# Layer 1 of a two-layer diffusion backbone: queries and keys leave the projection already turned, values are projected first

## The chip, the core and the metric

The kernel runs on one core of one Trainium2 chip. The metric is the device time of one execution in microseconds (us). Five engines work on their own instruction streams and wait for each other by semaphores: TensorE (PE, matmuls and turns), VectorE (DVE), ScalarE (ACT), GpSimd (POOL, which here only issues DMAs) and SyncE (SP, which issues the loads of all large weights).

## The reference

One step of a backbone with two layers over 384 tokens of width 1024: 128 context tokens (tile t=0) and 256 latent tokens (tiles t=1 and t=2), the latter on a grid of 4 rows and 64 columns. Layer 0 runs grouped-query attention and an mLSTM side by side; layer 1 runs neighbourhood attention. Behind each follows a mixture of experts (32 experts, two a token). Everything is float32. The change is in layer 1's mixer, which in the reference is

```python
q, k, v = split(h @ w_in, 3)            # h: 384 x 1024, w_in: 1024 x 3072; 16 heads of 64
# context tokens: plain attention over the 128 context tokens
# latent tokens: one softmax over
#   s_win = q . k(window) * scale + bias[head, drow, dcol]    (4 rows x 16 columns around the query)
#   s_ctx = q . cached_k * scale                              (128 cached context keys)
o = p_win @ v(window) + p_ctx @ cached_v
x = x + gate * (o @ w_out)
# further outputs: new_na_k, new_na_v = k and v of the context tokens
```

`h` is the normed and modulated row of x, with the modulation from a linear map of the condition.

## The kernel before

All weights go through a ring of six places of 2 MB each; SP issues the loads in the order of the list `stream`, each as soon as the place's former user is done (`freed`). Both layers share one set of functions; an argument `l` says which layer it is. In every function each engine works its list strictly in order.

**Turns of the normed rows.** At the end of layer 0, VectorE adds the experts' output to x and norms row tile after row tile (`rows`, `combine`, `normed`), announcing each by `h_ready`. ScalarE does the squares for it (`finish_layer`). PE turns each tile by eight 128x128 transposes (`transpose_rows`, L509), and ScalarE copies them from two banks into `hT` (`copy_transposed`, L1035). ScalarE comes to these copies only when the squares of all three tiles are done, and PE begins the projection only when all three tiles are turned.

**Projection** (`project`, L528). Six chunks of 512 columns of `w_in`: two of queries, two of keys, two of values. For each chunk and each token tile a group of eight accumulating matmuls: the stationary operand is a 128x128 block of `hT`, the moving one 512 columns of weights. The groups go round over four banks (banks 2 to 5); VectorE copies the even ones, ScalarE the odd ones (`copy_projected`), into rows of `qkv[1]`: token in the partition, column along the row. The bias table is masked by VectorE between two of its copies (`window_bias`).

**Attention** (`attention`). Eight pairs of heads, three units a pair (one for each token tile), 24 units in a pipeline over four engines:
- `scores` on PE (L701): two heads, 128 queries against 128 keys (t=0) or 384 keys (cached, then latent).
- `find_max` on VectorE: for latent units the max over cached keys (L1271), then bias sum and max over the 256 latent keys of each head (L1576).
- exponentials on ScalarE (L1134), scaling by the sum on VectorE (`normalise`, L1588 and L1591).
- `turn_probs` on PE (L714), copy on ScalarE (L1124), `values` on PE (L737), heads out by VectorE (`take_heads`, L1601).

The scores need queries and keys with the head's dimension in the partition. So for every pair PE turns its queries (`turn_queries`, L670 and L672: three blocks; those of latent tokens by a matmul with the table `flip`, which also mirrors the 64 columns of each grid row) into bank 7, ScalarE scales and copies them to `qT` (L1111), PE turns the keys (`turn_keys`, L686: four blocks) into the same bank, and VectorE copies them to `kT` (L1274). For the first pair this stands ahead of all units; for pair j+1 the queries are turned behind the values of pair j's first unit, the keys behind those of its second. Eight pairs, so the last pair has no turns of a following one beside it. The heads of the latent tokens are mirrored back by `take_heads`.

**POOL's queue in layer 1**: 32 loads of the bias table behind the last `h_ready`, the cached keys when all rows are turned, the cached values when the projection is done (they go where `hT` was), then both outputs `new_na_k` and `new_na_v`, then what waits for the end of attention.

**Output projection** (`project_out`, L786) takes the heads, which lie turned already, as stationary operand.

Of the kernel before, what the change touches and what calls it, by code (L numbers as in the profile page):

```python
# [24 lines left out]
P = 128  # L25
# [46 lines left out]
for _name, _n in (("ident", 128), ("trif", 128), ("ones", 128), ("flip", 128), ("window", 64),  # L72
                  ("slot", 128), ("skip", 1), ("eps", 1), ("pair", 3)):
    KEEP[_name] = slice(_at, _at + _n)
    _at += _n
# [9 lines left out]
def tables():  # L85
# [8 lines left out]
    mirror = p - col + GRID_W - 1 - col  # L94
    keep[p, KEEP["flip"].start + mirror] = 1.0
# [25 lines left out]
def build(nc, a, o):  # L121
    ctx = ExitStack()
    with ctx:
# [27 lines left out]
        def small_cut(*shape):  # L151
# [5 lines left out]
            if len(shape) == 3:  # L157
# [9 lines left out]
        ident, trif, ones, flip = (keep[:, KEEP[n]] for n in ("ident", "trif", "ones", "flip"))  # L167
        h = area_h[:, :].rearrange("p (t d) -> p t d", t=NT)
        hT = area_t[:, :].rearrange("p (k n) -> p k n", k=KT)
        qkv = [area_q[:, 0:NT * AB_W].rearrange("p (t n) -> p t n", t=NT),  # L170
               area_q[:, :].rearrange("p (t n) -> p t n", t=NT)]
# [29 lines left out]
        qT = [v.rearrange("p (b n) -> p b n", b=2) for v in (area_h[:, 1536:2304], area_h[:, 0:768])]  # L201
        kT = [v.rearrange("p (b n) -> p b n", b=2) for v in (area_t[:, 0:1024], area_h[:, 768:1792])]
        na_k = area_h[:, 1792:2816]
# [50 lines left out]
            "pair_done", "qT_copied", "kT_copied", "scores_done", "max_ready", "prob_ready", "prob_scaled", "probT_done",  # L254
# [29 lines left out]
        FIRST = (0, 2, 1, 3)  # L284
        stream = [("ada", 0, c) for c in FIRST[0:2]] + [("in", 0, 0)] + [("ada", 0, c) for c in FIRST[2:4]]
# [4 lines left out]
        for l in range(2):  # L290
            if l:
                stream += [("in", 1, c) for c in range(NA_CHUNKS)]
# [3 lines left out]
        IN_CHUNKS = (AB_CHUNKS, NA_CHUNKS)  # L296
        IN_W = (AB_W, NA_W)
        PROJ0 = (0, AB_CHUNKS * NT)

# [7 lines left out]
        def freed(eng, n):  # L307
# [5 lines left out]
            if kind == "in":  # L313
                eng.wait_ge(S["proj_done"], PROJ0[l] + NT * (c + 1))
# [45 lines left out]
        def _(sp):  # L360
# [65 lines left out]
            for n in range(NUM["in", 1, 0], NUM["moe", 1, 0]):  # L426
                if n == NUM["in", 1, 1]:
# [8 lines left out]
        def _(pe):  # L436
# [75 lines left out]
            def project(l):  # L512

                for c in range(IN_CHUNKS[l]):
                    if l == 0 and c == 0:
                        project_first()
                        continue
                    n = NUM["in", l, c]
                    w = min(512, IN_W[l] - 512 * c)
                    pe.wait_ge(landed[place(n)], when(n))  # L520
                    for t in range(NT):
                        g = PROJ0[l] + NT * c + t
                        if c == 0:
                            pe.wait_ge(S["trans_copied"], 2 * (NT * 2 * l + t + 1))
                        if g >= 4:
                            pe.wait_ge(S["proj_copied_act" if g % 2 else "proj_copied_dve"], (g - 4) // 2 + 1)
# [4 lines left out]
                    if l == 0:  # L531
                        ada_step(("in", c))

            def mlstm():

                for n in range(2 * NT):
# [6 lines left out]
                    for hh in range(B_HEADS):  # L543
                        c0 = (BK if side else BQ) + hh * BD
                        mm = pe.transpose(banks[3 + side][:, hh * P:hh * P + P], qkv[0][:, t, c0:c0 + BD], ident)
# [41 lines left out]
                def number_products(v, d):  # L587
                    pe.wait_ge(S["amatT_copied"], v + 1)
                    for hh in range(B_HEADS):
                        mm = pe.matmul(banks[5][:, hh * P:hh * P + P], amatT[:, hh, :],  # L590
                                       qkv[0][:, STAGES[s][d], BV + hh * BD:BV + hh * BD + BD], start=True, stop=True)
# [3 lines left out]
                for s in range(3):  # L595
# [28 lines left out]
                    if s < 2:  # L624

                        for d in range(2):
                            pe.wait_ge(S["kw_ready"], v + d + 1)
                            for hh in range(B_HEADS):
                                mm = pe.matmul(banks[(3, 0)[d]][:, hh * P:hh * P + P], kw[d][:, hh, :],
                                               qkv[0][:, STAGES[s][d], BV + hh * BD:BV + hh * BD + BD],  # L630
# [21 lines left out]
            def turn_queries(l, j):  # L652

                if l == 0 and j == 0:
                    pe.wait_ge(S["kdup_ready"], 1)
                    pe.wait_ge(S["ctx_v"], 16)
                if l == 1 and j == 0:
                    for name in ("proj_copied_dve", "proj_copied_act"):
# [1377 lines left out]
```

## Time and profile before

| what | us |
|---|---|
| median of 3 runs | 1692.09 (1684.51 to 1694.17) |
| the profiled execution | 1688.97 |
| its span (first to last instruction) | 1687.1 |
| PE busy | 1522.2 (90%) |
| VectorE, ScalarE, GpSimd busy | 450.8, 304.6, 145.8 |
| layer 1's rows turned (first turn to projection) | 886.13 to 897.3 |
| layer 1's projection | to 1022.54 |
| layer 1's attention | to 1099 |

PE records overlap (a pass of 512 columns is recorded with 592 ns while the next one starts 429 ns later), so PE's busy time is no measure of how dense its work is. The chain of waits is the sequence of work that ended last, followed back from the last instruction; "issue" in it is time in which an engine waited for nothing that the profile shows.

### The profile page before, as it was taken

The numbers are of one execution on the slowest core, as the hardware profiler recorded it, in microseconds if no ns is written. First come the engines' busy times: TensorE is split into PE (matmuls) and PEld (weight loads), VectorE is DVE, ScalarE is ACT, GpSimd is POOL, SyncE is SP. The second block draws the span as 40 slices with busy tenths as digits, with TensorE's granted clock in tenths as the row PEclk, the third lists the DMA queues.
The fourth block names the chain that finished last, engine by engine and source line by source line (L and its number), as shares of the span: only waits on it lengthen the run. The fifth ranks groups of instructions, "written<-read, shape, count | busy, mean of one in ns | idle before, by whom it ended". The sixth has DMA issues, their size and how long they took to land.

```text
span 1687.1 us, 21430 instructions
## 1 busy us (share of the span) xinstructions
PE 1522.2 (90%) x8379; PEld 718.6 (43%) x8379; DVE 450.8 (27%) x1061; ACT 304.6 (18%) x637; POOL 145.8 (9%) x200
## 2 busy tenths in 40 slices
PE   5999877978999999999948998896999999999991
PEld 3455765444433333333314444544433333334340
DVE  0012576434111111111132025733311111111113
ACT  3100224211111111111121004611111111111112
POOL 1002102100000000000005000010000000000001
PEclk9999978978999999999988999997999999999996
DMA  9898953234999999999969322023899999999982
GB/s 349 295 343 181 384 203 126 80 161 199 428 428 428 429 427 428 428 428 427 427 253 303 143 100 88 2 79 137 341 428 428 427 428 427 428 429 427 428 357 116
DMA packets 82919, 521.63 MB, mean 309 GB/s; under 512 B 10130, under 2 KB 11610, under 8 KB 56240
## 3 DMA queue, kind: packets, MB, share of 16 engines
q1 hardware_dynamic: 69536, 485.58, 70.5%
q0 software_dynamic: 13328, 35.29, 6.8%
q8 instruction: 38, 0.62, 0.2%
q14 instruction: 17, 0.14, 0.0%
HBM read 511.08 MB, written 20.22 MB: 315 GB/s over the span
## 4 chain that ended last, share of the span: by engine, by line
PE 86%; DVE 9%; ACT 1%; DMA 1%; issue 1%; POOL 0%; DVEq 0%; POOLq 0%; ACTq 0%
PE psum L840 25%; PE psum L853 14%; PE psum L528 13%; PE psum L821 10%; PE psum L786 5%; PE psum L846 3%; PE psum L452 2%; PE psum L833 2%; PE psum L827 2%; PE psum L494 1%; PE psum L714 1%; PE psum L701 1%; DVE area_q L1261 1%; DVE area_m L1261 1%; PE psum L737 1%
## 5 line engine op out<-in xcount | busy, mean ns | idle before, releaser
L840 PE MATMUL psum<-ring,area_t 128*64 128x512 f32 x1024 | 450.0, 592 | 2.2 <-issue 1.2
L841 PE MATMUL psum<-ring,area_t 128*64 128x512 f32 x1024 | 450.3, 592 | 0.0
L840 PEld LDWEIGHTS psum<-ring,area_t 128*64 128x64 f32 x1024 | 139.7, 137 | 291.5 <-issue 291.3
L853 PE MATMUL psum<-ring,area_t 128*64 128x512 f32 x1024 | 233.8, 598 | 2.2 <-DVE area_t L1758 2.2
L528 PE MATMUL psum<-ring,area_t 128*128 128x512 f32 (+1 forms) x528 | 220.0, 578 | 0.0
L1729 DVE COPY area_q<-psum 64x512 f32<-64x512 f32 x64 | 44.5, 695 | 568.6 <-PE psum L841 568.5
L821 PE MATMUL psum<-area_h,area_t 128*64 128x512 f32 x768 | 180.7, 606 | 3.0 <-DVE area_t L1743 3.0
L528 PEld LDWEIGHTS psum<-ring,area_t 128*128 128x128 f32 x528 | 100.5, 191 | 116.1 <-issue 114.3
L1940 POOL DMA_INDIRECT pair_rows<-area_q,idx x64 | 62.4, 975 | 931.6 <-ACT area_q L1176 931.6
L841 PEld LDWEIGHTS psum<-ring,area_t 128*64 128x64 f32 x1024 | 139.7, 137 | 0.0
L853 PEld LDWEIGHTS psum<-ring,area_t 128*64 128x64 f32 x1024 | 68.5, 136 | 122.0 <-issue 122.0
L1166 ACT ACTIVATE area_q<-psum 64x512 f32<-64x512 f32 x64 | 37.8, 590 | 404.5 <-PE psum L841 404.5
L821 PEld LDWEIGHTS psum<-area_h,area_t 128*64 128x64 f32 x768 | 57.3, 140 | 113.1 <-issue 109.8
L1176 ACT COPY area_q<-psum 128x512 f32<-128x512 f32 x64 | 37.4, 585 | 278.9 <-PE psum L853 278.9
L786 PE MATMUL psum<-ring,area_q 128*128 128x512 f32 x192 | 87.6, 618 | 0.0
L1758 DVE TENSOR_TENSOR area_t<-psum,area_t 128x256 f32<-128x256 f32 x64 | 27.2, 425 | 182.5 <-ACT area_t L1171 182.5
L1274 DVE COPY area_q<-psum 128x512 f32<-128x512 f32 (+2 forms) x20 | 12.6, 629 | 205.2 <-PE psum L528 193.3
L1156 ACT COPY area_q<-psum 128x512 f32<-128x512 f32 x64 | 37.4, 585 | 137.1 <-PE psum L821 137.1
L846 PEld LDWEIGHTS psum<-keep,area_q 128*128 128x128 f32 x256 | 35.8, 209 | 53.7 <-issue 50.3
L786 PEld LDWEIGHTS psum<-ring,area_q 128*128 128x128 f32 x192 | 37.9, 199 | 46.8 <-issue 46.8
L1045 ACT COPY area_q<-psum 128x512 f32<-128x512 f32 (+1 forms) x18 | 10.1, 563 | 230.7 <-PE psum L528 223.7
L1735 DVE COPY area_t<-psum 128x512 f32<-128x512 f32 x64 | 44.3, 692 | 27.9 <-PE psum L827 27.9
(252 smaller groups left out, 1341.8 us busy)
## 6 DMA issues: line engine op xcount, KB each, us to landing
ring<-in_moe_w SPq DMA_DIRECT2D x192, 2048.0 KB, 15.9
ring<-in_ada_w SPq DMA_DIRECT2D x24, 2048.0 KB, 20.0
ring<-in_na_w_in SPq DMA_DIRECT2D x6, 2048.0 KB, 17.4
ring<-in_ab_w_in SPq DMA_DIRECT2D x5, 2048.0 KB, 18.4
area_m<-mod_ready POOLq DMA_DIRECT2D x6, 1024.0 KB, 9.4
area_q<-pair_rows POOLq DMA_DIRECT2D x6, 1024.0 KB, 7.2
ring<-in_ab_w_out SPq DMA_DIRECT2D x2, 2048.0 KB, 19.6
area_g<-mod_ready POOLq DMA_DIRECT2D x4, 1024.0 KB, 8.4
```

The costliest lines, as they stand in the source:

```text
L528: mm = pe.matmul(banks[2 + g % 4][:, 0:w], hT[:, k, t * P:t * P + P], wchunk(n, KT)[:, k, 0:w], start=(k == 0), stop=(k == KT - 1))
L786: mm = pe.matmul(banks[2 + g % 2][:, :], qkv[l][:, t, c0 + k * P:c0 + k * P + P], wchunk(n, KT)[:, k, :], start=(k == 0), stop=(k == KT - 1))
L821: mm = pe.matmul(banks[0][64 * half:64 * half + 64, :], pick[:, 0:BLOCK], h[:, t, 512 * half:512 * half + 512], start=(n == 0), stop=(n == ...
L840: pe.matmul(banks[2 + u][0:64, :], lhsT, w1[:, k, :], start=(k == 0), stop=(k == KT - 1))
L841: mm = pe.matmul(banks[2 + u][64:128, :], lhsT, w3[:, k, :], start=(k == 0), stop=(k == KT - 1))
L846: mm = pe.transpose(banks[4][:, k * P:k * P + P], hs[u][:, k:512:4], ident)
L853: mm = pe.matmul(banks[6 + u][64 * j:64 * j + 64, :], hidT[u][:, k, :], w2[:, k, 512 * j:512 * j + 512], start=(k == 0), stop=(k == 3))
L1156: act.copy(tok, banks[0][:, :]).then_inc(M["tok_copied"], 1)
L1166: act.activation(hs[u][0:64, :], banks[2 + u][0:64, :], ACT.Silu).then_inc(M["silu_done"], 1)
L1729: v.tensor_copy(hs[u][64:128, :], banks[2 + u][64:128, :]).then_inc(M["up_copied"], 1)
L1735: v.tensor_copy(xT[u][:, :, :].rearrange("p k s -> p (k s)"), banks[1][:, :]).then_inc(M["xT_copied"], 1)
L1940: pool.indirect_dma_start(out=pair_dram[l], in_=ysb[u], in_offset=None, out_offset=bass.IndirectOffsetOnAxis(ap=idx[u][:, :], axis=0), bou ...
```

## The change

In layer 1 the groups of queries and keys swap the two operands of the matmul: the stationary one is a 128x128 block of the weights (one pair of heads), the moving one is `hT` with all 384 tokens. What comes out is the pair's queries or keys with the head's dimension in the partition. The copy of the group scales the queries and mirrors their latent part (a reversed access pattern), so `turn_queries`, `turn_keys`, their copies and the table `flip` go for layer 1. Values stay as they were. There are 6 groups of values (512 columns) and 16 of queries and keys (384 columns), in the order `NA_ORDER`: values, values, queries, keys, queries, keys. The first group of values (t=0) stands between the turn of tile 0 and those of tiles 1 and 2; ScalarE copies a turned tile before it leaves `finish_layer`.

The keys of each pair lie in their own 512 columns, new ones first, cached ones behind; the cached keys are turned by `turn_na`: those of pairs 0 to 3 ahead of the projection's last chunk (copied by VectorE), those of pairs 4 to 7 in attention behind unit 3 (copied by ScalarE). Since `new_na_k` is wanted in rows, the context's keys are turned back behind units 6 and 9 and copied by ScalarE. On POOL, the cached keys no longer wait for the turned rows, `new_na_v` is stored when its values are copied, and `new_na_k` behind the last of these turns; VectorE waits for it before the norm of tile 2 behind the output projection. The bias table is masked behind group 14. The first scores wait for the last copies. Layer 0 keeps its order.

```diff
+        NA_ORDER = (4, 5, 0, 2, 1, 3)
+        NA_GROUPS = [(c, n) for c in NA_ORDER for n in range(NT if c >= 4 else 4)]
+        PROJ_END = PROJ0[1] + len(NA_GROUPS)
+        NA_CACHED_AT = (1, 3)
+        WINDOW_AT = PROJ0[1] + 14
+        NA_TURNS_AT = {3: 1, 6: 2, 9: 3}
+            def project_na():
+                for g, (c, i) in enumerate(NA_GROUPS, PROJ0[1]):
+                    n = NUM["in", 1, c]
+                    w = wchunk(n, KT)
+                    if c == NA_ORDER[0]:
+                        for t in ((0,), (1, 2), ())[i]:
+                            transpose_rows(2, t)
+                        pe.wait_ge(S["trans_copied"], 2 * (NT * 2 + i + 1))
+                    if i == 0:
+                        pe.wait_ge(landed[place(n)], when(n))
+                    bank_free(g)
+                    for k in range(KT):
+                        if c >= 4:
+                            mm = pe.matmul(banks[2 + g % 4][:, :], hT[:, k, i * P:i * P + P], w[:, k, :],
+                                           start=(k == 0), stop=(k == KT - 1))
+                        else:
+                            mm = pe.matmul(banks[2 + g % 4][:, 0:TOKENS], w[:, k, i * P:i * P + P], hT[:, k, :],
+                                           start=(k == 0), stop=(k == KT - 1))
+                    mm.then_inc(S["proj_done"], 1)
+                    if (c, i) == NA_CACHED_AT:
+                        turn_na(0)
+            def turn_na(n):
+                if n == 0:
+                    pe.wait_ge(S["na_ctx_loaded"], 16)
+                else:
+                    pe.wait_ge(S["na_copied"], n)
+                for b in range(4):
+                    j = 4 * (n % 2) + b
+                    src = na_k[:, P * j:P * j + P] if n < 2 else na_kT[j][:, 0:P]
+                    mm = pe.transpose(banks[7][:, P * b:P * b + P], src, ident)
+                mm.then_inc(S["na_turned"], 1)
...
             def attention(l):
-                turn_queries(l, 0)
-                turn_keys(l, 0)
+                if l == 0:
+                    turn_queries(0)
+                    turn_keys(0)
...
+                    if l == 1 and i in NA_TURNS_AT:
+                        turn_na(NA_TURNS_AT[i])
...
+            def copy_na():                      # ScalarE, odd groups; VectorE has the same for even ones
+                    if c >= 4:
+                        step(act.copy(na_vals[:, i, 512 * (c - 4):512 * (c - 3)], src[:, :]), "proj_copied_act")
+                    elif c >= 2:
+                        step(act.copy(na_kT[4 * (c - 2) + i][:, 0:TOKENS], src[:, 0:TOKENS]), "proj_copied_act")
+                    else:
+                        q = na_q[:, 4 * c + i, :]
+                        step(act.mul(q[:, 0:P], src[:, 0:P], HD ** -0.5), "act_step")
+                        step(act.mul(q[:, P:TOKENS].rearrange("p (r c) -> p r c", r=ROWS), mirrored(src[:, P:TOKENS], ROWS),
+                                     HD ** -0.5), "proj_copied_act")
...
+                def copy_turned(n):
+                    act.wait_ge(S["na_turned"], n + 1)
+                    if n < 2:
+                        for b in range(4):
+                            ins = act.copy(na_kT[4 * n + b][:, TOKENS:512], banks[7][:, P * b:P * b + P])
+                        step(ins, "na_copied")
+                    else:
+                        step(act.copy(na_krows[:, 512 * (n - 2):512 * (n - 1)], banks[7][:, :]), "na_copied")
...
                     squares(t)
+                    if l == 0 and t:
+                        copy_transposed(2, t - 1)
+                if l == 0:
+                    copy_transposed(2, NT - 1)
...
-                    pool.wait_ge(S["trans_done"], 2 * NT * 3)
                     get(na_k, a["cache_na_k"][0, 0].rearrange("t h d -> t (h d)"), "na_ctx_loaded")
-                    pool.wait_ge(S["proj_done"], PROJ0[1] + NA_CHUNKS * NT)
+                    for name in ("proj_copied_dve", "proj_copied_act"):
+                        pool.wait_ge(S[name], (PROJ0[1] + 2 * NT) // 2)
+                    get(o["new_na_v"][0, 0].rearrange("t h d -> t (h d)"), na_vals[:, 0, :], "kv_stored")
+                    pool.wait_ge(S["proj_done"], PROJ_END)
                     get(na_v, a["cache_na_v"][0, 0].rearrange("t h d -> t (h d)"), "na_v_loaded")
+                    pool.wait_ge(S["na_copied"], 4)
+                    get(o["new_na_k"][0, 0].rearrange("t h d -> t (h d)"), na_krows, "kv_stored")
```

## Rows read from the trace of the kernel before

**Rows 1.** The page's first lines: the span, and the granted clock in 40 slices.
```profile
span 1687.1 us, 21430 instructions
...
PEclk9999978978999999999988999997999999999996
```

**Rows 2.** Timeline, 879 to 898 us: start, length, engine, line, operation, what ended the idle time.
```profile
879.73 15.05 SPq L364 DMA_DIRECT2D ring<-in_na_w_in  x5
...
886.13 1.97 PE L509 MATMUL psum<-keep,area_h 128*128 128x128 f32 x8 [21.16 <-DVE area_h L1261]
...
891.33 1.05 ACT L1035 COPY area_t<-psum 128x512 f32<-128x512 f32 x2
...
894.24 1.23 DVE L1261 TENSOR_TENSOR area_h<-area_h,area_m 128x1024 f32<-128x1024 f32 x1
...
895.52 1.97 PE L509 MATMUL psum<-keep,area_h 128*128 128x128 f32 x8 [0.81 <-DVE area_h L1261]
```

**Rows 3.** Windows: stretch, length, busy time of PE, PEld, DVE, ACT, POOL; PEclk, DMA, GB/s.
```profile
889.00:892.70 3.70, 0.00 (x0) 0.00 (x0) 3.58 (x4) 2.40 (x5) 0.00 (x0) 0.50 1.05 387
...
897.50:900.00 2.50, 2.50 (x4) 0.95 (x4) 0.00 (x0) 0.58 (x1) 2.50 (x5) 0.50 1.06 391
900.00:905.00 5.00, 5.00 (x13) 2.27 (x12) 0.00 (x0) 0.00 (x0) 5.00 (x9) 0.97 1.06 273
```

**Rows 4.** Timeline within layer 1's projection.
```profile
984.61 37.93 PE L528 MATMUL psum<-ring,area_t 128*128 128x512 f32 x88
...
989.04 9.46 DVE L1261 TENSOR_TENSOR area_m<-area_m,keep 128x384 f32<-128x384 f32 x16
```

**Rows 5.** Chain of waits, layer 0's last two chunks (512, then 272 columns).
```profile
138.52 20.80 PE psum L528 x48
...
162.94 11.20 PE psum L528 x48
```

**Rows 6.** Chain of waits, start of layer 1's attention: start, length, what.
```profile
1022.54 0.72 issue
...
1026.15 0.49 PE psum L701 x4
...
1027.05 0.85 PE psum L670 x4
1027.90 1.61 PE psum L701 x4
...
1029.53 0.44 DVE small L1271
...
1032.37 0.43 DVE small L1271
```

**Rows 7.** Timeline of the same start.
```profile
1024.56 1.28 ACT L1134 ACT_TABLE_LOAD   x1
...
1026.75 0.42 DVE L1569 TENSOR_REDUCE small<-psum 128x2 f32<-128x256 f32 x1 [0.70 <-PE psum L701]
...
1031.06 0.16 DVE L1588 RECIPROCAL small<-small 128x2 f32<-128x2 f32 x1
```

**Rows 8.** Chain of waits in attention: a keys' turn, the third units' max of the last two pairs.
```profile
1039.30 0.59 PE psum L686 x4
...
1083.24 0.44 DVE small L1271
...
1090.36 0.44 DVE small L1271
```

**Rows 9.** Windows: the last pair period with turns, and the one without.
```profile
1074.76:1083.24 8.48, 7.44 (x65) 4.85 (x64) 6.86 (x26) 5.53 (x16) 0.00 (x0) 1.00 0.01 3
1083.24:1090.36 7.12, 6.08 (x55) 3.78 (x55) 6.26 (x25) 4.71 (x14) 0.00 (x0) 1.00 0.00 0
```

**Rows 10.** Groups by form in attention: ScalarE, with count, busy us and mean ns.
```profile
L1134 ACT ACTIVATE area_g<-psum,small 128x128 f32<-128x128 f32 x16 | 5.8, 369 | 1.4 <-DVE small L1569 1.4
L1111 ACT ACTIVATE area_h<-psum 128x384 f32<-128x384 f32 x8 | 4.0, 495 | 0.9 <-PE psum L670 0.9
```

**Rows 11.** DMA issues: KB each, us from issue to landing.
```profile
area_t<-in_cache_na_v POOLq DMA_DIRECT2D x1, 512.0 KB, 10.9
```

More of the change, by code:

```diff
@@ L700, in scores @@
                     rows = slice(64 * hh, 64 * hh + 64)
-                    mm = pe.matmul(psum[:, 2 * (U % 2) + hh, 0:k1 - k0], qT[l][rows, g % 2, t * P:t * P + P],
-                                   kT[l][rows, g % 2, k0:k1], start=True, stop=True)
+                    mm = pe.matmul(psum[:, 2 * (U % 2) + hh, 0:k1 - k0], q[rows, t * P:t * P + P],
+                                   keys[rows, k0:k1], start=True, stop=True)
                 mm.then_inc(S["scores_done"], 1)
@@ L784, in project_out @@
                         for k in range(KT):
-                            c0 = BQ - 512 if (l == 0 and k >= 4) else 0
-                            mm = pe.matmul(banks[2 + g % 2][:, :], qkv[l][:, t, c0 + k * P:c0 + k * P + P],
+                            c0 = (BQ - 512 if k >= 4 else 0) + k * P
+                            turned = ab[:, t, c0:c0 + P] if l == 0 else na_q[:, k, t * P:t * P + P]
+                            mm = pe.matmul(banks[2 + g % 2][:, :], turned,
                                            wchunk(n, KT)[:, k, :], start=(k == 0), stop=(k == KT - 1))
@@ L1141, in attention @@
                         act.wait_ge(S["bout_turned"], t + 1)
-                        step(act.copy(qkv[0][:, t, BQ:BQ + 512], banks[7][:, :]), "bout_copied")
+                        step(act.copy(ab[:, t, BQ:BQ + 512], banks[7][:, :]), "bout_copied")
             def route(l):
@@ L1347, in normed, with copy_ab @@
                 tt(out, out, plus, ALU.add, "h_ready")
[L1349 to L1350 removed]
+            def copy_ab():
+                for g in range(0, AB_CHUNKS * NT, 2):
+                    c, t = divmod(g, NT)
+                    w = min(512, AB_W - 512 * c)
+                    v.wait_ge(S["proj_done"], g + 1)
+                    cp(ab[:, t, 512 * c:512 * c + w], banks[2 + g % 4][:, 0:w], "proj_copied_dve")
+                    if g == 2 * NT:
+                        head_squares()
+                    if g == 4 * NT + 2:
+                        head_norms()
+                    if (c, t) in ((3, 1), (5, 1)):
+                        modulation(c // 2)
@@ L1364, in copy_projected @@
+                    if g == WINDOW_AT:
                         window_bias()
+                v.wait_ge(S["na_turned"], 1)
+                for b in range(4):
+                    ins = v.tensor_copy(na_kT[b][:, TOKENS:512], banks[7][:, P * b:P * b + P])
+                do(ins, "na_copied")
             def gate_logs():
@@ L1597, in take_heads @@
                     v.wait_ge(S["pv_done"], U + 1)
-                    heads = banks[6][:, 0:P]
-                    if l == 1 and t:
-                        heads = heads.rearrange("p (r c) -> p r c", r=2)[:, :, ::-1]
-                    v.tensor_copy(qkv[l][:, t, P * j:P * j + P], heads).then_inc(S["heads_out"], 1)
-                copy_keys(0)
+                    heads, out = banks[6][:, 0:P], ab[:, t, P * j:P * j + P]
+                    if l == 1:
+                        out = na_q[:, j, t * P:t * P + P]
+                        if t:
+                            heads = mirrored(heads, 2)
+                    v.tensor_copy(out, heads).then_inc(S["heads_out"], 1)
+                if l == 0:
+                    copy_keys(0)
                 for i in range(NU[l] + 3):
```

256 lines of the change are left out of this document (125 added, 131 removed).

## The prediction

> **What bounds the kernel now.** I read the page from the top: span and slices first, then the chain of waits from 840 to 1300 us, then the timeline and the table of windows for the stretches that the change touches. The page shows TensorE (PE) busy nearly everywhere at a granted clock of 0.9 and more, with dips at the borders of stages [rows 1]. So a stage gets shorter only if PE work or a PE wait on the chain goes. The change touches three stretches of layer 1.
>
> First, the turns of the normed rows. PE turns t=0 at 886.13, then has nothing until t=1 is ready at 892.7 and t=2 at 895.47, and begins the projection behind the third turn, at 897.49 [rows 2]. In all of this the clock is at 0.50 (1.2 GHz) and it stays there into the projection; it is back at full only at about 900.2: still 0.50 from 897.5 to 900, then 0.97 on average to 905 [rows 3]. Second, the projection itself, 288 passes (an f32 matmul leaves two), PE without a pause until 1022.54, 429.2 ns a pass: (37.93 - 0.59) / 87 [rows 4, 6]. Third, attention, 1022.54 to 1099. It begins with turns and their copies, the next pair's turn falls into a low clock, and the max of unit 1 starts 7.0 us after the projection's end, that of unit 2 9.83 us after [rows 6]. Then eight pairs of heads follow; from one pair's third unit to the next pair's it is (1083.24 - 1032.37) / 6 = 8.48 us, six times, and 7.12 us the last time [rows 6, 8]. That last pair is the only one beside which nothing is turned for a following pair. Loads play no part: no chain piece in these stretches is a DMA.
>
> **The projection.** 48 value matmuls of 512 columns stay as they are; the other 96 become 128 of 384 columns, with the weights as stationary operand. Columns in all: 144 x 512 = 73,728 before and 48 x 512 + 128 x 384 = 73,728 after. A pass of 384 columns is not in the trace, but the same line ran 48 passes of 512 in 20.80 us and 48 of 272 in 11.20 us in layer 0 [rows 5]: 433 and 233 ns, 0.833 ns a column, straight through a floor of about 2.5 ns once the 0.2 us of the switch is taken off. So 384 columns are 322.5 ns. 256 x 0.3225 + 80 x 0.4292 = 82.56 + 34.34 us for everything behind the first group. Bounds: 322.5 and 429.2 ns (the 512-column pass, if a pass had a price of its own); I take the first, because 272 columns already lie below it.
>
> **Values between the turns.** ScalarE now copies the turned row t before it leaves the layer's end, where today it waits for all three squares (its first copy is at 891.33, over 3 us behind the turn [rows 2]). The first turn ends at 888.1, the second copy at about 888.8. Group 0 (values, t=0: 16 passes, 6.87 us at full clock) then starts in what is a wait today. How fast it goes hangs on the clock: today the clock rose 4.7 us after PE began to run without a gap (895.52 to 900.2) [rows 2, 3]. From 888.8 that gives 893.5: 2.35 us' worth of work before it and 4.52 behind, end at 898.0. Both other rows are long ready by then, so their turns follow at full clock: 2 x 2 x 0.59 (0.59 for four blocks [rows 8]) and 0.1 for a bank that is being copied: 2.46. With the turn of the cached keys that is put before the last chunk (0.59 + 0.07) the projection ends at 898.0 + 2.46 + 34.34 + 82.56 + 0.66 = 1018.0 instead of 1022.54: **4.5 us less**. Bounds: 1.1 if the clock rises when it does today (900.2, group 0 ends at 901.4), 5.8 if it counts from the first turn (890.8). I take the middle one since it repeats today's distance.
>
> The copies of the groups (VectorE and ScalarE take turns, four banks) are now due every 5.2 us instead of 6.9, so 10.3 on each engine: 0.50 us for 128x384 [rows 10]; a mirrored one is two smaller instructions, and even at twice the price it has room. The bias sum on VectorE (16 instructions, 9.46 us [rows 4]) sits behind group 14 and ends before that engine's next group is done. The weights come in the new order through SP's same queue: five loads are issued from 879.73 on [rows 2] at 387 GB/s [rows 3], 5.4 us for 2 MB, and the first of these is needed at 898.0 + 2.46 + 13.7 = 914.
>
> **The start of attention.** Removed: turn of the queries, its copy, turn of the keys, its copy. With T the projection's end: the last copy is 128x384 on ScalarE (0.50 [rows 10]; today one of 128x512 takes 0.08 more and PE goes on 0.72 behind T [rows 6]), so the scores of unit 0 start at T+0.64. VectorE begins the max 0.60 later (1026.15 to 1026.75 [rows 6, 7]) and ends at T+1.66. The table load of 1.28 us [rows 7], hidden today, starts behind the copy and ends at T+1.84, so unit 0's exponentials (2 x 0.37 and a read [rows 10]) are done at T+2.75 and unit 2's scores at T+3.6. Unit 1's scores are behind unit 0's, and its max starts at T+2.0; it takes 1.53 us (1029.53 to 1031.06 [rows 6, 7]), unit 0's scaling 0.60, and unit 2's max starts at T+4.2 against T+9.83: 5.6 us less. Two costs of today's low clock (the second turn 0.85 instead of 0.45, scores 1.61 instead of 0.87, [rows 6]) may come again, since PE still has gaps here: then 4.4. I take **5.0**. A third bound: cached values are asked for at T and landed 10.9 us later today [rows 11], with a weight load and both outputs beside them. They are first needed at about T+10.3, so if nothing is faster 0.9 us is lost: 3.5. But one output now leaves earlier and the other later, so I take no stall.
>
> **The pairs.** Six times 8.48 become six times the turnless 7.12 [rows 6, 8]: **8.2 us**. The chain agrees: queries' turn 0.71 and the keys' turn and copy 0.6 are what stands in it beyond the last pair's pieces. Bounds: 4.3 if the key half was off the path in the middle pairs, 8.2 at the top. The value is the one that a row shows.
>
> **Added in attention.** Three turns of four blocks (cached keys 4 to 7, then the new keys back to rows for the output), where queries were turned before: 3 x 0.59 = **1.8 us more**. Their copies are ScalarE's: four of 128x128, 0.37 each by its other instruction of that size [rows 10], or one large one. Behind them on ScalarE stands the copy of turned probabilities, and PE finishes these only 1.7 us later (scores and turns, 0.87 each). Bounds 0 and 3.0 (if the four copies are waited for). The output of keys leaves after the third pair, and the wait for it in front of t=2's norm is 40 us later: nothing.
>
> Sum: 4.5 + 5.0 + 8.2 - 1.8 = 15.9 us. The profiled execution took 1688.97 us (span 1687.1 and 1.9 around it); after: 1673.1. The median of the runs shown is 3.1 above the profile, so I forecast **1676.2** for a median. Everything behind (output projection, experts) is released by PE and shifts as a whole. Bounds together: 1.1 + 3.5 + 4.3 - 3.0 = 5.9 less, to 5.8 + 5.6 + 8.2 = 19.6 less.
>
> **A rule against a row.** With the turns gone, PE does less per pair, and the clock could see that. In the turned pair and in the turnless one it is 1.00, with PE busy 7.44 of 8.48 and 6.08 of 7.12 us [rows 9]. The Trainium skill, "TensorE: Matmul & The Clock Gate", section "Part 4: PE-mode transpose", says that a transpose doesn't count as work for the clock. By it the removed turns never held the clock up, and the rival below has no ground; if they count, the one turnless pair is the only witness. The trace can't tell which; the sum is the same by both.
>
> **Rivals.** (a) The clock falls to 1.2 GHz in layer 1's attention, since gaps remain and turns are gone. At half clock 6.08 us of PE work become 12.16 [rows 9], 5.0 over the period; eight pairs cost 40, net 24 slower: 1716 on the median's scale. It decides from 15.9 / 5.0 = 3.2 pairs on. Against it: the turnless pair at 1.00. 3 in 100. (b) Weights as stationary operand: a 384-column pass keeps 429.2 ns. 256 x 0.107 = 27.3 more, net 11.4 slower, 1703.5; it decides from 62 ns more a pass. Against it: 272 columns at 233 ns [rows 5]. 2 in 100. (c) Values gain nothing in the gap, the clock rising when it does today, and the start's slow clock and the late cached values take the rest: 1.1 + 3.5 + 8.2 - 1.8 = 11.0 less, 1681. For it: the clock is low at both places today. 15 in 100. (d) The change does only half in the pairs, VectorE or the latency of the exponentials holding them, and (c) too: 5.9 less, 1686, which is no measurable change. Against it: the last pair. 8 in 100. My own case has 72.
>
> **Range and chances.** Below 0.5% (8.4 us) a measurement of this kernel can't tell a gain from none. 8 in 10 lie between 1670 (19.6 less and the spread of the runs) and 1685 (between c and d). Faster: 72 + 15 = 0.87; same 0.08; slower 0.05.
>
> **What would show it.** Group 0 of the values between 888.8 and 898; full clock by 894; projection over at 1018 with 322 ns a pass; unit 2's max about 4.8 us behind that; pairs of 7.1 us, three of them 0.6 longer; clock 1.00 there. It is wrong if passes of 384 columns take over 350 ns, if pairs stay above 8 us, or if the clock is at 0.50 past the start of attention.

## The result, and the profile after

The changed kernel has a median of 1678.59 us (7 runs, 1675.94 to 1679.88). The kernel before, beside it, has 1688.82 (7 runs, 1684.51 to 1694.23). The ratio is 0.9928 [0.9912, 0.9943], so it is faster by 0.7%. Two repeats in other sessions, each beside its own runs of the kernel before, gave 0.9894 [0.9876, 0.9913] and 0.9907 [0.9892, 0.9922]. The forecast of 1676.2 for 1692.09 is a ratio of 0.9906. In microseconds the gain of the medians is 10.2 here and 18.2 and 15.9 in the repeats, against 15.9 forecast. All times are of fast executions, but for one of the five with matmuls in experiment 4 (1733.47 us at a granted clock of 0.906), which is in its median and not in its ratio.

The profiled execution took 1678.59 us. The first lines of its page show a span 10.3 us shorter and dips of the clock in much the same places as before [rows 1]:

```profile
span 1676.8 us, 21435 instructions
...
PEclk9999977987999999999998999997999999999995
```

The chain of waits of the changed kernel, from the first turn of the normed rows to the fifth pair (start, length, what). It answers to [rows 2, 4, 6, 8]:

```profile
889.27 1.98 PE psum L524 x8
...
891.91 9.28 PE psum L562 x16
901.18 0.45 PE psum L524 x4
...
902.39 1.06 PE psum L524 x8
903.45 34.34 PE psum L562 x80
937.79 61.92 PE psum L565 x192
999.71 0.44 PE psum L580 x4
1000.14 20.64 PE psum L565 x64
1020.79 0.61 issue
1021.40 1.15 PE psum L740 x8
1022.58 0.44 DVE small L1343
...
1024.78 0.34 DVE small L1343
...
1027.22 1.54 PE psum L753 x6
...
1030.43 1.58 PE psum L740 x4
...
1034.90 0.44 DVE small L1343
...
1042.62 0.44 DVE small L1343
...
1050.32 0.44 DVE small L1343
...
1057.44 0.44 DVE small L1343
```

Read from top to bottom: the first group of values (L562 x16) stands between the turns. Then PE runs on without a gap for 117.3 us. A pass of 384 columns takes 61.92 / 192 = 0.3225 us. The max of unit 2 starts at 1024.70 (the chain enters it at 1024.78), 3.91 us behind the projection's end at 1020.79. The next third units' max follow at 1034.90, 1042.62, 1050.32 and 1057.44: pairs of 10.20, 7.72, 7.70 and 7.12 us.

The windows of the changed kernel (columns as in [rows 3]) show the clock in the gap, then at the start of attention, then in a pair without any turn:

```profile
895.00:897.00 2.00, 2.00 (x4) 0.72 (x3) 1.93 (x3) 0.00 (x0) 0.00 (x0) 0.69 1.05 385
897.00:899.00 2.00, 2.00 (x6) 0.88 (x5) 1.57 (x2) 0.00 (x0) 0.00 (x0) 1.00 1.05 385
...
1024.00:1026.00 2.00, 1.31 (x10) 0.53 (x6) 1.90 (x9) 1.50 (x5) 0.00 (x0) 0.99 0.99 420
1026.00:1028.00 2.00, 0.90 (x6) 0.79 (x5) 1.78 (x9) 1.23 (x4) 0.00 (x0) 0.50 0.93 393
1028.00:1030.00 2.00, 2.00 (x11) 1.34 (x10) 0.85 (x3) 1.21 (x4) 0.00 (x0) 0.50 0.38 154
1030.00:1032.00 2.00, 2.00 (x8) 0.59 (x6) 0.00 (x0) 1.08 (x6) 0.00 (x0) 0.50 0.03 8
1032.00:1034.00 2.00, 2.00 (x22) 1.66 (x20) 1.83 (x9) 0.76 (x2) 0.00 (x0) 0.80 0.00 0
...
1050.32:1057.44 7.12, 6.14 (x55) 3.85 (x56) 6.26 (x25) 5.08 (x16) 0.00 (x0) 1.00 0.06 24
```

The clock falls to 0.50 at about 1026, in the first pair, and comes back at about 1032.8, 6.8 us later. In that stretch the same probabilities' turns (L753 x6) take 1.54 us instead of 0.88 and the scores (L740 x4) 1.58 instead of 0.84. This is what makes the first pair 10.20 us long.

By stage, both profiled executions (S is the first turn of the rows, T the projection's end, O the start of the output projection):

| stage | before | after | difference | forecast |
|---|---|---|---|---|
| all before S | 886.13 | 889.27 | +3.1 | 0 |
| S to T | 136.41 | 131.52 | -4.9 | -4.5 |
| T to unit 2's max | 9.83 | 3.91 | -5.9 | -5.0 |
| unit 2's max to unit 23's | 57.99 | 54.10 | -3.9 | -8.2 + 1.8 |
| unit 23's max to O | 8.63 | 7.32 | -1.3 | 0 |
| O to the end | 588.11 | 590.68 | +2.6 | 0 |

The stretch that was changed, S to O, is 16.0 us shorter, against 15.9 forecast (15.1 and 15.8 in the traces of the two repeats). Around it, where PE's instructions are the same, this execution was 5.7 us longer. In front, the difference lies in the first units of layer 0's attention. The chain of the kernel before there, then that of the changed one:

```profile
278.70 0.88 PE psum L714 x6
```

```profile
278.56 1.54 PE psum L753 x6
```

The same work at the same moment, once at full clock and once at 1.2 GHz. In a second profiled execution of the changed kernel (experiment 1), the clock was 1.00 from 274 to 286. From the last matmul ahead of layer 0's attention to its output projection this kernel took 46.06 us in the first trace and 43.81 and 42.85 in those of the repeats; the kernel before took 42.87. So this is a difference between executions, not between kernels.

Behind O the difference goes with the clock too. TensorE was at half clock for 59.8 us of O to the end in the trace of before (588.1 us), for 67.1 in this one (590.7), and for 61.6 and 67.1 in those of the repeats (588.9 and 590.7).

### The profile page after: what moved, and what is told of

It is laid out like the page before. It is cut to its first block, busy times and chain, and to the rows that moved or that the text cites. A ratio compares the mean times of both kernels' runs of the same rounds, so it can differ in the third digit from the quotient of the medians.

```text
span 1676.8 us, 21435 instructions
## 1 busy us (share of the span) xinstructions
PE 1519.0 (91%) x8387; PEld 724.7 (43%) x8387; DVE 447.8 (27%) x1063; ACT 303.6 (18%) x641; POOL 145.8 (9%) x200
## 4 chain that ended last, share of the span: by engine, by line
PE 86%; DVE 9%; ACT 2%; DMA 1%; issue 1%; POOL 0%; DVEq 0%; POOLq 0%; ACTq 0%
PE psum L885 26%; PE psum L898 14%; PE psum L866 10%; PE psum L543 6%; PE psum L831 5%; PE psum L565 5%; PE psum L891 3%; PE psum L562 3%; PE psum L467 2%; PE psum L878 2%; PE psum L872 2%; PE psum L509 1%; PE psum L753 1%; PE psum L740 1%; DVE area_m L1333 1%
## 5 line engine op out<-in xcount | busy, mean ns | idle before, releaser
L543 PE MATMUL psum<-ring,area_t 128*128 128x512 f32 (+1 forms) x240 | 94.7, 554 | 0.0
L565 PE MATMUL psum<-area_t,ring 128*128 128x384 f32 x256 | 82.9, 486 | 0.0
L543 PEld LDWEIGHTS psum<-ring,area_t 128*128 128x128 f32 x240 | 45.2, 190 | 46.8 <-issue 45.0
L565 PEld LDWEIGHTS psum<-area_t,ring 128*128 128x128 f32 x256 | 48.6, 190 | 33.9 <-issue 0.5
```

The costliest lines, as they stand in the source:

```text
L543: mm = pe.matmul(banks[2 + g % 4][:, 0:w], hT[:, k, t * P:t * P + P], wchunk(n, KT)[:, k, 0:w], start=(k == 0), stop=(k == KT - 1))
L565: mm = pe.matmul(banks[2 + g % 4][:, 0:TOKENS], w[:, k, i * P:i * P + P], hT[:, k, :], start=(k == 0), stop=(k == KT - 1))
```

## The experiments

**1. The same kernel again, with the gap part undone.** Both ran on one chip, five runs each, beside nine runs of the kernel before (median 1691.67). First the changed kernel itself:

> The changed kernel once more, for a second trace. In its first one the stretch from the first turn of the normed rows to the output projection was 16 us shorter than before, but 2.9 us were lost in layer 0's attention and 2.5 in layer 1's first pair of heads, each with the granted clock at 0.50. Theory P: these falls come and go between executions (nothing of layer 0's code changed), so at least one of the two is at full clock here and the pieces are back at 283 us for layer 0's 6th unit and 7.7 us for the first pair. Theory S: they belong to the new kernel, and both are there again within 0.5 us. Time 1678 by either, within 3.

Measured: 1673.48 us (1670.71 to 1679.21), ratio 0.9894 [0.9876, 0.9913]. Its stages: S to T 132.15, to unit 2's max 3.91, first pair 10.48, then 7.71, 7.70 and 7.12. Of the two low clocks the one in layer 0's first units was not there this time, as theory P has it; the one in the first pair was, as theory S has it, and it came again in a third trace (10.28). So the slow first pair is no accident of one execution.

```diff
-                        for t in ((0,), (1, 2), ())[i]:
+                        for t in ((0, 1, 2), (), ())[i]:
                             transpose_rows(2, t)
```

> The changed kernel with one part undone: all three normed rows are turned before the first group of values, which no longer stands in the wait between them. Theory: the part is worth 4.9 us (by the two traces, 136.4 against 131.5 us from the first turn to the projection's end), so 1683.5. Rival: the clock rises as early through the turns alone, or the time is taken back by a low clock at the start of attention: within 1.5 us of the changed kernel.

Measured: 1680.15 us (1678.32 to 1683.17), ratio 0.9922 [0.9909, 0.9936]: 6.7 us above the changed kernel's median on the same chip. Its chain of waits shows the projection behind all three turns and in one piece:

```profile
898.56 1.97 PE psum L524 x8
900.53 43.06 PE psum L562 x96
...
1026.59 0.61 issue
```

S to T is 137.42 here, 5.3 to 5.9 more than in the three traces of the changed kernel. The gap part is worth that much up to T, and the rival of a gain under 1.5 us is out. Behind T nothing was changed, and still the first pair takes 9.22 and not 10.2 to 10.5: the clock was low for 3.4 us in it, not for 6.8.

```profile
1034.00:1036.00 2.00, 2.00 (x10) 1.33 (x11) 0.65 (x3) 1.83 (x8) 0.00 (x0) 0.50 0.30 119
1036.00:1038.00 2.00, 2.00 (x12) 0.76 (x9) 0.77 (x2) 0.37 (x3) 0.00 (x0) 0.69 0.04 8
```

**2. The gap part alone**, in the kernel before: values first, the first group between the turns, the copies in `finish_layer`.

```diff
+        ORD = (tuple(range(AB_CHUNKS)), (4, 5, 0, 1, 2, 3))
...
-                stream += [("in", 1, c) for c in range(NA_CHUNKS)]
+                stream += [("in", 1, c) for c in ORD[1]]
...
-                        if c == 0:
+                        if pos == 0:
+                            for tt in ((0,), (1, 2), ())[t]:
+                                transpose_rows(2, tt)
                             pe.wait_ge(S["trans_copied"], 2 * (NT * 2 * l + t + 1))
```

> The kernel before with that part alone: values are projected first, group 0 between the turns, ScalarE copies the turned rows earlier; queries and keys are still projected in rows and turned pair by pair. Theory: 4 to 5 us faster than before, 1684.5 on the scale of a median of 1688.8, and the projection ends 131 us behind the first turn. Rival: it needs the rest of the change, for instance because the cached keys or the weights come too late in the new order: no gain.

Measured: 1683.19 us (1682.64 to 1683.71), ratio 0.9945 [0.9931, 0.9958], 8.5 below the kernel before. Its chain at the gap and at the projection's end, and its window where the clock rises:

```profile
886.15 1.96 PE psum L510 x8
...
888.76 9.18 PE psum L531 x16
897.94 0.45 PE psum L510 x4
```

```profile
1016.94 0.72 issue
```

```profile
892.00:893.00 1.00, 1.00 (x2) 0.34 (x1) 0.93 (x3) 0.00 (x0) 0.00 (x0) 0.54 1.05 387
```

S to T is 1016.94 - 886.15 = 130.79: 5.6 less than before. The pairs stay at 8.48, but for the first, which is 10.05. Unit 2's max comes 8.53 behind T here, 9.83 before: in the kernel before the slow stretch lay ahead of that max (scores of 1.61 us, [rows 6]), here it lies behind it, 3.4 us long, and the first pair is 1.6 longer. So the slow first pair belongs to the place and not to the new attention. Experiments 1 and 2 agree on the gap part up to T: 5.3 to 5.9. The medians give 6.7 and 8.5, with all that the clock does elsewhere in them.

**3. Turns put back into the pairs**, into a bank that nobody reads: three blocks behind a pair's first unit, four behind its second (in pairs that have a turn of the cached keys, only the other half).

```diff
                     if l == 1 and i in NA_TURNS_AT:
                         turn_na(NA_TURNS_AT[i])
+                    elif l == 1 and i < NU[1] - NT and i % NT < 2:
+                        pe.wait_ge(S["na_copied"], 1 + sum(at < i for at in NA_TURNS_AT))
+                        for b in range(3 if i % NT == 0 else 4):
+                            pe.transpose(banks[7][:, P * b:P * b + P], na_q[:, b, 0:P], ident)
```

> The changed kernel with PE's turns put back beside pairs 0 to 6 and nothing else: three blocks behind the first unit's values and four behind the second's, into bank 7, whose content nobody reads; no copies by ScalarE and VectorE. Theory: both turns stand in the chain of a pair, 0.45 to 0.48 for three blocks and 0.5 to 0.59 for four, so a pair goes from 7.12 to 8.1 and the kernel loses 6 us: 1684.5. Rival: the copies (0.50 and 0.68 us) made the old pair 8.48, the PE turns alone fit into gaps: pairs stay below 7.5, under 2 us lost.

Measured: 1677.05 us (1675.11 to 1678.74), ratio 0.9906 [0.9891, 0.9921]; 3.6 above the changed kernel on that chip. A window at the start of attention, two pieces of its chain, and then the turns of a pair in the chain of the kernel before:

```profile
1025.00:1027.00 2.00, 1.26 (x11) 0.93 (x12) 1.84 (x6) 1.45 (x5) 0.00 (x0) 1.00 0.71 289
```

```profile
1051.86 0.48 PE psum L813 x3
...
1054.79 0.59 PE psum L813 x4
```

```profile
1044.61 0.26 PE psum L672
1044.87 0.45 PE psum L670 x4
...
1047.77 0.59 PE psum L686 x4
```

Pairs take 8.17 to 8.30 us, as the theory says. From 7.12 the shortest is 1.05 us more, and the added pieces are 0.48 + 0.59 = 1.07. In the kernel before a pair took 1.36 more (8.48), and its turns are 0.26 + 0.45 + 0.59 = 1.30 in the chain: the blocks of the latent queries are matmuls with `flip`, two passes each, so that three blocks take 0.71 there and 0.48 here. So nearly all of the 1.36 is PE time of the turns, and the wait for their copies is 0.06 at most; the rival, by which the copies made the pair long, is out. The kernel lost 3.6 us in the median and not the 6 that were expected, since the first pair shows something new: it is 8.28 and not 10.5, with the clock at 1.00. The added turns kept the clock up.

**4. The start of attention kept busy.** Three kernels ask what holds the clock in the first pair. The first one only moves the three added turns from units 3, 6, 9 to units 0, 1, 2. The second and the third put work without a reader behind the scores of units 1, 2 and 3: 4, 2 and 5 matmuls of 128 columns (two passes each), or twice as many transposes (one pass each).

```diff
-        NA_TURNS_AT = {3: 1, 6: 2, 9: 3}
+        NA_TURNS_AT = {0: 1, 1: 2, 2: 3}
```

```diff
                         scores(l, i)
+                    if l == 1:
+                        for _ in range({1: 4, 2: 2, 3: 5}.get(i, 0) * 1):
+                            pe.matmul(banks[7][:, 0:P], trif, ident, start=True, stop=True)
```

> The changed kernel with the three turns of cached and new keys moved from units 3, 6 and 9 to units 0, 1 and 2, where PE has gaps while the first unit goes round the other engines. In the changed kernel the clock is at 0.50 from about 5 to 12 us behind the projection's end and the first pair takes 10.2 to 10.5 us (7.7 for the second). Theory (sparse PE work there lets the clock fall, and work of any kind prevents it): first pair 7.2 to 8, pairs two and three 7.12 instead of 7.70, in all 3.5 to 4.5 us faster than the changed kernel's 1673.5. Rival (ScalarE is the bound at the start: its copies of the turned blocks, up to 1.2 us, delay the first exponentials, and the fall comes anyway): the 1.2 us of the two later pairs at most, or nothing.

> The changed kernel with 11 matmuls of 128x128 by 128x128 (two passes each, some 0.21 us a matmul at full clock, 2.4 us in all) that compute nothing of use, behind the scores of units 1, 2 and 3 of layer 1 (4, 2 and 5 of them), where PE waits. Theory: the clock stays at 1.00 and the first pair goes from 10.3 to 8: 2 us faster. Rival: the fall is decided by something else than PE's work there: first pair 10.3 or longer by what does not fit into the gaps.

> As the last one, with 22 transposes of 128x128 in the same places instead of 11 matmuls (one pass of about 0.11 to 0.15 us each, 2.4 to 3.2 in all). If a transpose counts for the clock like a matmul, as the kernel with the pairs' turns put back suggests (clock 1.00 over the whole first pair, 8.29 us with two turns), the same 2 us are gained; if it does not count, the first pair stays at 10.3 or grows.

Windows of the kernel with transposes, then of that with matmuls, then of that with the turns moved:

```profile
1025.00:1027.00 2.00, 2.00 (x20) 1.55 (x17) 1.85 (x7) 1.45 (x5) 0.00 (x0) 1.00 0.88 369
```

```profile
1022.00:1024.00 2.00, 2.00 (x19) 1.54 (x17) 1.72 (x6) 1.45 (x5) 0.00 (x0) 1.00 0.86 354
```

```profile
1025.00:1027.00 2.00, 1.66 (x10) 0.64 (x8) 1.79 (x8) 1.38 (x5) 0.00 (x0) 1.00 0.97 410
```

All three stay at 1.00. The kernel before aside, where it fell ahead of the pair, the clock fell in the first pair in the six traces without added work at this place (three of the changed kernel, those of experiments 1 and 2 and of the kernel with a fill in layer 0 alone), and in none of the five with it. By their traces, from T to unit 23's max:

| kernel | T to unit 2's max | pairs | sum |
|---|---|---|---|
| before | 9.83 | 8.48 x6 and 7.12 | 67.8 |
| changed | 3.91 | 10.20, 7.72, 7.70, 7.12 x4 | 58.0 |
| fill, matmuls | 3.90 | 7.70, 7.71, 7.71, 7.12 x4 | 55.5 |
| fill, transposes | 3.91 | 7.70, 7.70, 7.71, 7.12 x4 | 55.5 |
| turns moved | 4.89 | 7.12 x7 | 54.7 |

So the slow first pair costs 2.5 us and is PE's clock alone, the extra work itself costs nothing there, and a turn beside a pair costs 7.71 - 7.12 = 0.59. With the turns moved, unit 2's max comes 1.0 us later, since ScalarE's copies of the turned keys (0.67 in the chain) stand in front of it. What the fills gained they lost in part at the very end of attention. The chain of the kernel with transposes, then that of the changed one:

```profile
1078.89 1.11 PE psum L753 x6
1080.01 1.50 PE psum L778 x12
```

```profile
1083.18 0.85 PE psum L753 x6
1084.03 0.83 PE psum L778 x12
```

From unit 23's max to the output projection it is 8.62 us with either fill, as before (8.63), and 7.32 in the changed kernel. The medians don't resolve the rest: 1674.23 (turns moved, 0.990 [0.9886, 0.9914]), 1673.29 (matmuls, 0.990 [0.9886, 0.9914]) and 1673.54 (transposes, 0.9909 [0.9890, 0.9928]), beside 1690.07 for the kernel before. The changed kernel's own repeats lie at 0.9894 and 0.9907. So the gains of 2 and of 3.5 to 4.5 us that were expected are there in the traces up to unit 23's max (2.5 and 3.3), up to the output projection they are 1.2 and 3.3, and in the times they are not shown.

**5. Layer 0's start of attention, and both together.** The +3.1 us in front of S suggested the same medicine for layer 0: 4, 2 and 4 matmuls without a reader around the first turns of queries and keys, 5 behind the scores of unit 3.

```diff
                 if l == 0:
+                    fill(4)
                     turn_queries(0)
+                    fill(2)
                     turn_keys(0)
+                    fill(4)
...
+                    if l == 0 and i == 3:
+                        fill(5, 6)
```

> The changed kernel again, beside the two below. 1673 to 1679, layer 1's first pair 10.2 to 10.5 us with the clock at 0.50 for some 6 us of it, as in both traces so far. Layer 0's attention ends anywhere between 307 and 314.6 us, as it did over eight traces of kernels whose layer 0 is the same.

> The changed kernel with 15 idle matmuls (128x128 by 128x128, 3.2 us at full clock) in the gaps at the start of layer 0's attention: 4 before the first turn of queries, 2 before the first turn of keys, 4 behind it, 5 behind the scores of unit 3. Theory: the spread of layer 0 (7 us between traces) is the same fall of the clock after sparse work, and filling takes it away: layer 0's attention always ends near the lower end, 307 to 309 us, and the kernel is 2 to 4 us faster in the median than the changed kernel. Rival: the clock is already low from what runs before 262 us (0.50 to 0.9 in every trace), so the idle matmuls only cost their up to 3.2 us.

> Both: the three turns of keys at units 0 to 2 of layer 1's attention, and the idle matmuls at the start of layer 0's. If both theories hold, 3.6 us from layer 1 (seen in the trace of the kernel with early turns alone: 54.7 against 58.3 us from the projection's end to the last unit's max) and 2 to 4 from layer 0: 1667 to 1669. If layer 0's part fails: 1671 to 1675.

Measured, beside 1691.44 for the kernel before: the changed kernel 1675.56 (1672.54 to 1679.88; 0.9907 [0.9892, 0.9922]), with the fill in layer 0 1669.97 (1669.37 to 1674.27; 0.9880 [0.9865, 0.9895]), with the moved turns as well 1670.60 (1665.14 to 1671.58; 0.9865 [0.9848, 0.9882]). Both medians lie 5 to 6 us below the changed kernel's on this chip. The interval of the kernel with both edits doesn't meet the changed one's, that of the fill alone does by a little, and whether the moved turns add to the fill can't be told.

Layer 0's stretch doesn't explain it. The windows of the kernel with the fill, then one of the kernel with both:

```profile
270.00:274.00 4.00, 4.00 (x30) 2.93 (x30) 3.65 (x12) 2.84 (x9) 0.00 (x0) 1.00 0.89 377
...
292.00:296.00 4.00, 3.34 (x14) 1.82 (x14) 3.83 (x10) 1.38 (x6) 0.00 (x0) 0.50 0.00 0
```

```profile
298.00:302.00 4.00, 3.45 (x14) 1.87 (x14) 3.83 (x10) 1.37 (x6) 0.00 (x0) 0.50 0.00 0
```

The fill did keep the clock at 1.00 where it stands. But 6.8 us at half clock came later, near 292 and near 298, as much in all as in the trace of the changed kernel beside them (two stretches of 3.4 us, from 272.4 and 296.3). The last matmuls ahead of this stretch, in the changed kernel, with the fill and with both:

```profile
265.78 2.46 PE L467 MATMUL psum<-ring,cond 128*32 128x128 f32 x84
```

```profile
261.79 1.92 PE L467 MATMUL psum<-ring,cond 128*32 128x128 f32 x64
```

```profile
267.73 1.91 PE L467 MATMUL psum<-ring,cond 128*32 128x128 f32 x62
```

They end at 268.24, 263.71 and 269.64, and layer 0's output projection begins at 311.09, 305.95 and 311.58. Of the 5.1 us by which the kernel with the fill is ahead there, 4.5 lie in front of its first added matmul; the stretch itself takes 42.25 and 41.94 us with the fill and 42.85 without. That is 0.6 to 0.9 less, and up to 4 less than in other traces of the changed kernel (46.06, 43.81). The kernel with both edits gained nothing up to there; its trace is 4.4 shorter than the changed kernel's chiefly by layer 1's start of attention (T to unit 23's max 54.7 instead of 58.1) and by O to the end (588.9 instead of 590.7). So the theory that the fill makes layer 0's attention always end near 307 to 309 failed, and what made the median of the kernel with the fill alone lower is open.

## Why the prediction was right, and where it was off

The direction, the size and the parts' order came out, and the measured 1678.59 and the repeats' 1673.48 and 1675.56 lie in the range. But the 16.0 us of the trace equal the 15.9 of the forecast only because four misses cancel, and that is luck. By the medians of the first session alone (10.2 us less) rival (c) with its 11.0 would fit better than the forecast's own case; it is the stages of the traces that decide between them.

**Projection.** A pass of 384 columns was to take 322.5 ns, and it does; rival (b) is out. The 256 passes and the 80 of values took 82.56 and 34.34 us, as forecast, without a wait for a weight load. The copies had room: straight ones of 384 columns took 479 ns on ScalarE and 558 on VectorE, the mirrored ones, in two instructions, 278 + 378 and 292 + 424.

**Values between the turns.** Forecast -4.5, measured -4.9 in this trace, -4.3 and -4.7 in the repeats' traces. The cached keys' turn in the projection (0.44) is in that; the gap part by itself was forecast at 4.5 + 0.66 = 5.2 and gave 5.3 to 5.9 in experiments 1 and 2. Group 0 was to end 11.9 us behind the first turn's start, and did (901.18 - 889.27). The clock was to be full 7.4 us behind that start. The window of 0.69 over 895 to 897 puts it at 896.2, so 7.0; in the kernel of experiment 2 it is 6.8, by 0.54 over 892 to 893, and in the traces of the repeats 8.3 and 7.3. The rival (c) for this part, a clock that rises no earlier than before, is out: [rows 3] had it 14 us behind the first turn. The two later turns with the wait between them were to take 2.46 us and took 2.27 (903.45 - 901.18).

**Start of attention.** Forecast -5.0 with -4.4 if the low clock comes again, measured -5.9. Scores start 0.61 us behind T (forecast 0.64), unit 1's max at 1.79 (2.0), unit 2's at 3.91 (4.2). The 0.6 us that I had set aside for the low clock weren't needed there. The late cached values cost nothing, as taken: they landed 9.1 us after their issue.

**The pairs: the step that failed.** I took "1.00 there" from a pair in the middle [rows 9] and counted six pairs at 7.12, three of them 0.6 longer. Five of the six are exactly that (7.72, 7.70, 7.12, 7.12, 7.12). The first is 10.20, 2.5 too long. The low clock that I had charged to the start of attention was not there but in the pair behind it: with the start shorter, the slow stretch lay behind unit 2's max and not ahead of it. The prediction had named the low clock as a risk for the start of attention (4.4 instead of 5.6 there), and a clock at 0.50 past the start as a sign of being wrong. That sign came, in one pair: it cost 2.5 us, since it lasts 6.8 us and PE works at half speed with hardly a pause in it. Rival (a), the clock at half in all eight pairs for 40 us, came true in this one pair alone; rival (d), pairs that shorten by half, is out by the pairs of 7.12. Experiment 4 shows the cause as far as it can be shown: with PE's idle time filled, by whatever work, the clock stays at 1.00, the pair takes 7.70, and the pairs' total is 51.6, which is 6.4 less than before: the forecast's 8.2 - 1.8. The reason for the 8.2 was right as well: the turns' PE time, by experiment 3. The prediction counted the copy of the keys in it, and that was not in the chain: the turns alone are 1.30 of the 1.36 us.

**The rule against the row.** The prediction left open whether transposes hold the clock up. Here they did: the kernel with transposes as its only fill had a granted clock of 1.00 where the changed one had 0.50, and the same pairs as the kernel with matmuls (7.70, 7.70, 7.71). By the Trainium skill, "TensorE: Matmul & The Clock Gate", section "Part 4: PE-mode transpose", transposes don't count as work for the clock; the traces here disagree, and the measurement decides. Nor would the rule have covered all that was removed: two of the seven blocks of a pair were matmuls with `flip`. The sum took the clock at 1.00 by either reading, and the first pair, where PE had fewer turns than before and paused, is where it was not.

**Behind the pairs.** I let all this shift as a whole. It is 1.3 us less from unit 23's max to the output projection, where PE turned and multiplied at full clock in this kernel (0.85 and 0.83 us) and at a lower one with the fills (1.11 and 1.50). The repeats of the changed kernel have 7.32 both, and so has the kernel of experiment 2, whose attention is the old one: so this gain is not the new attention's. The kernels with the gap part undone and with either fill in layer 1 have 8.62 or 8.63. Why the clock falls there in some kernels and not in others is open.

**The time.** The median is 2.4 above the forecast. The forecast started from 1692.09, and seven runs of the kernel before gave 1688.82, which alone would put it 3.3 lower; the gain was 5.7 less than forecast. The traces have the same 5.7 around the stretch that was changed: 3.1 in front of it, in layer 0's start of attention at half clock, and 2.6 behind O, where the kernels do the same. O to the end is 588.1 to 590.7 in all kernels run, and it goes with the time at half clock in it: 588.1 with 59.8 us, 588.7 to 589.3 with 61 to 64, 590.4 to 590.7 with 67. The forecast, by which everything behind shifts as a whole, left this out. In the second session the trace as a whole is 16.9 below the first trace of before.

## What to carry to other kernels

A change that removes waits leaves the slow stretches of TensorE's clock where the idle time is, and they can move into the next stage and take part of the gain: look at the granted clock of the stage behind the one that is changed, not only at a settled repetition in its middle. Where PE waits on other engines for a few microseconds, give it work that is due anyway (the turns of later heads here) or work without a reader; either kept it at full clock there. But look at where the clock falls next: with the fills it fell at the end of attention instead, and in layer 0 some 20 us behind them, and took back a part or all of the gain. Compare such an edit with several traces of the same kernel, from the last instruction ahead of it: one that starts 4.5 us earlier by itself looks like a success. And read the parts of the sum one by one: a total that fits to 0.1 us held four errors between 0.4 and 2.5.

## What the runs showed of the hardware

- An f32 pass takes the same time by column whichever operand is the weight: 429.2 ns at 512 columns with `hT` stationary (34.34 / 80), 322.5 at 384 with the weights stationary (61.92 / 192); that is 0.838 and 0.840 ns a column.
- A mirrored read (negative step) out of PSUM is hardly dearer than a straight one: 378 ns for 128x256 on ScalarE (scaled in the same instruction), where a straight copy of that size takes 372.
- After the fall at about 1026 the clock stayed at 0.50 for 6.8 us, though PE was busy without a gap for most of it (2.00 of 2.00 us in two windows).
- Twenty-two transposes held the clock up as well as eleven matmuls with twenty-two passes: 1.00 in both and first pairs of 7.70 us, against 0.50 and 10.20 without either.
- In twelve traces PE's work from O to the end is the same, and the stretch takes 588.1 to 590.7 us: the shortest with 59.8 us at half clock, the longest with 67.1.
